# Expert weights in 2 MB transfers and paired slots, in a two-layer trunk kernel on one core

## The reference

```python
def reference(x, ...):
    for l in range(DEPTH):                      # DEPTH = 2
        h = rmsnorm(x, mix_norm_g[l])
        z = h @ w_in[l]                         # 1024 x 8192
        q, k, v, ch, cb, cc, ga, gc = jnp.split(z, offs, axis=-1)
        ...
        a = diff_attention(q, k, v, bias_dist, lam, lam_init, subln_g[l])
        c = short_gated_conv(ch, cb, cc, conv_w[l])
        merged = sigmoid(ga) * (a @ w_o_attn[l]) + sigmoid(gc) * (c @ w_o_conv[l])
        x = x + merged @ w_o[l]
        h = rmsnorm(x, ffn_norm_g[l])
        if l % 2 == 0:
            f = swiglu(h, dense_w_gate_up[0], dense_w_down[0])     # FF_DENSE = 2816
        else:
            logits = h @ router_w[0]
            top_v, top_i = lax.top_k(logits, 2)
            gates = jax.nn.softmax(top_v, axis=-1)
            for e in range(8):                                     # FF_EXPERT = 3584
                f = f + cw[:, e:e + 1] * swiglu(h, w_gu[e], w_down[e])
        x = x + f
    return rmsnorm(x, final_norm_g)
```

## Time and profile before

| What | Value |
|---|---|
| median of three runs | 1671.43 us |
| the profiled execution, its own time | 1670.79 us |
| its span in the profile | 1669.0 us |
| busy: PE, DVE, ACT | 98%, 79%, 66% |
| bytes moved, mean rate | 488.74 MB, 293 GB/s |
| start of the experts' first matmul, end of their last | 761.91, about 1653.5 us |
| TensorE's granted clock | full nearly throughout |

### The profile page before, as it was taken

One profiled execution on the slowest core, in us unless ns is written; L12 is line 12 of the kernel. 1 busy time (PEld: TensorE's weight loads), 2 busy tenths in 40 slices (PEclk: granted clock), 3 DMA queues, 4 the chain that ended last, 5 costly groups with the idle time before them and its releaser, 6 DMA issues.

```text
span 1669.0 us, 23179 instructions
## 1 busy us (share of the span) xinstructions
PE 1639.0 (98%) x8338; PEld 1373.9 (82%) x8338; DVE 1319.3 (79%) x1133; ACT 1102.0 (66%) x1076; POOL 225.6 (14%) x398
## 2 busy tenths in 40 slices
PE   9999999999999999999999999999999999999996
PEld 7988888888889888888888788887888887888875
DVE  6567656545465677468999999889999899998997
ACT  5355744444444557447768887778887688877885
POOL 0034440000000344407920000000000000000000
PEclk9999999999999999999999999999999999999998
DMA  8654544555545444536998999989999899999894
GB/s 339 264 177 152 187 179 164 202 184 193 179 173 177 169 159 171 188 147 254 412 379 348 417 421 401 409 334 397 421 398 418 348 374 419 419 399 379 341 422 199
DMA packets 71792, 488.74 MB, mean 293 GB/s; under 512 B 8651, under 2 KB 11932, under 8 KB 13212
## 3 DMA queue, kind: packets, MB, share of 16 engines
q1 hardware_dynamic: 69052, 483.89, 74.3%
q10 hardware_dynamic: 2656, 3.70, 0.7%
HBM read 484.94 MB, written 2.62 MB: 292 GB/s over the span
## 4 chain that ended last, share of the span: by engine, by line
PE 82%; DVE 9%; DMA 4%; issue 3%; ACT 1%; DVEq 0%; SPq 0%; ACTq 0%
PE bank L418 20%; PE bank L420 20%; PE bank L419 20%; DMA w_raw<-expert_slabs 3%; PE bank L1941 3%; PE bank L1942 3%; DVE w_lo L414 3%; PE bank L1722 3%; PE bank L1724 3%; PE bank L1725 3%; DVE e_v L411 2%; DVE e_uy L414 2%; PE bank L1920 2%; PE bank L1958 1%; DVE e_bias L414 1%
## 5 line engine op out<-in xcount | busy, mean ns | idle before, releaser
L414 DVE TENSOR_TENSOR w_lo<-w_raw,w_hi 128x2048 fp32r<-128x2048 f32 x288 | 654.5, 2292 | 210.2 <-ACT w_hi L405 209.8
L405 ACT ACTIVATE w_hi<-w_raw 128x2048 fp32r<-128x2048 f32 x288 | 551.2, 1918 | 389.3 <-PE bank L420 280.5
L418 PE MATMUL bank<-w_hi,hT 128*128 128x512 f32 x720 | 285.2, 396 | 1.9 <-DVE w_lo L1167 1.9
L420 PE MATMUL bank<-w_hi,hT 128*128 128x512 f32 x720 | 281.3, 391 | 0.0
L419 PE MATMUL bank<-w_lo,hT 128*128 128x512 f32 x720 | 280.8, 390 | 0.0
L418 PEld LDWEIGHTS bank<-w_hi,hT 128*128 128x128 f32 x720 | 135.5, 188 | 28.6 <-issue 2.1
L420 PEld LDWEIGHTS bank<-w_hi,hT 128*128 128x128 f32 x720 | 135.4, 188 | 28.7
L419 PEld LDWEIGHTS bank<-w_lo,hT 128*128 128x128 f32 x720 | 135.7, 188 | 26.8
L414 DVE TENSOR_TENSOR e_uy<-w_raw,e_k 128x2048 fp32r<-128x2048 f32 x56 | 128.2, 2288 | 16.7 <-ACT e_k L405 16.6
L411 DVE TENSOR_TENSOR e_v<-w_raw,hT 128x2048 fp32r<-128x2048 f32 x55 | 125.8, 2288 | 10.8 <-ACT hT L402 10.7
L405 ACT ACTIVATE e_k<-w_raw 128x2048 fp32r<-128x2048 f32 x56 | 107.5, 1920 | 34.3 <-PE bank L420 22.3
(11 more groups left out here) (355 smaller groups left out, 3125.9 us busy)
## 6 DMA issues: line engine op xcount, KB each, us to landing
w_raw<-expert_slabs SPq DMA_DIRECT2D x334, 1024.0 KB, 7.4
w_raw<-mix_slabs SPq DMA_DIRECT2D x88, 1024.0 KB, 4.8
w_raw<-dense_slabs SPq DMA_DIRECT2D x33, 1024.0 KB, 4.8
bias_lines<-bias ACTq DMA_DIRECT2D x1, 1536.0 KB, 7.5
X<-in_x SPq DMA_DIRECT2D x2, 512.0 KB, 5.8
bias<-bias_lines SPq DMA_DIRECT2D x1, 1024.0 KB, 6.8
yT<-in_ffn_norm_g ACTq DMA_DIRECT2D x2, 512.0 KB, 5.0
v_buf<-expert_slabs SPq DMA_DIRECT2D x1, 1024.0 KB, 4.7
```

What stands on the lines that cost most here:

```text
L405: act.activation(hi_slot(n), raw_of(n, early), ACT.Copy).then_inc(hi_ready, 1)
L414: eng.tensor_tensor(lo_slot(n), raw_of(n, early), hi_slot(n), ALU.subtract).then_inc(lo_ready, 1)
L418: pe.matmul(dst, hi, whi, start=first, stop=False, skip_group_check=True)
L420: return pe.matmul(dst, lo, whi, start=False, stop=last, skip_group_check=True)
```

## The change

Only the experts' stream changes its form; the mixers and the dense mixer still load halves. In the experts SP loads two halves with one transfer of 2 MB (`load_pair`) into two neighbouring slots of the same ring of six. ACT still makes the high parts half by half, but both wait for the one semaphore of the pair. DVE makes the low parts of both halves with one operation on 4096 floats a partition (`split_lo_pair`), which raises `lo_ready` by two. The slots of high and low parts become three pairs. `raw_slot` starts the experts' ring at slot 2. The loads into spare tiles in the opening are gone; the first pair is split in the mixer's last halves, the second behind the first gather. Beside this: the last dense step turns its last activations earlier and puts them in other tiles, `norm(2)` changes the order of two DVE operations, `rsqrt_of` loses one operation, and the end of the program works by halves of the columns, with the first rows scaled and sent by ACT.

```diff
-        w_hi = sb("w_hi", [P, SPLIT, HALF], F32R)
-        w_lo = sb("w_lo", [P, SPLIT, HALF], F32R)
+        w_split = sb("w_split", [P, 2 * SPLIT, HALF], F32R)
+        w_hi, w_lo = w_split[:, 0:SPLIT, :], w_split[:, SPLIT:2 * SPLIT, :]
...
+        moe_hi = (e_qv, w_split[:, 0:2, :], w_split[:, 2:4, :])
+        moe_lo = (e_bias, e_ku, w_split[:, 4:6, :])
...
+        def raw_slot(n):
+            return (n - MOE0 + 2) % RAW if n >= MOE0 else n % RAW
...
+        def load_pair(sp, n, src, cyc, opening=False):
+            at = raw_slot(n)
+            if opening and n < MOE0 + RAW:
+                sp.wait_ge(lo_ready, max(h for h in range(MOE0) if h % RAW in (at, at + 1)) + 1)
+            else:
+                sp.wait_ge(lo_ready, n - RAW + 2 + RAW * cyc)
+            sp.dma_start(w_raw[:, at:at + 2, :], src).then_inc(landed[at], 16)
...
         def split_hi(act, n, cyc=0):
+            slot, loads = raw_slot(n), n // RAW + 1
+            if n >= MOE0:
+                slot -= slot % 2
+                loads = loads_ahead(slot) + (n - MOE0) // RAW + 1
+            act.wait_ge(landed[slot], 16 * loads + 16 * cyc)
+            hi_slot_free(act, n, cyc)
+            act.activation(hi_slot(n), raw_of(n), ACT.Copy).then_inc(hi_ready, 1)
...
+        def split_lo_pair(eng, d, cyc=0):
+            def flat(pair):
+                return pair.rearrange("p h c -> p (h c)")
+
+            eng.wait_ge(hi_ready, MOE0 + 2 * d + 2 + RAW * cyc)
+            at = raw_slot(MOE0 + 2 * d)
+            eng.tensor_tensor(flat(moe_lo[d % SPLIT][:, :, :]), flat(w_raw[:, at:at + 2, :]),
+                              flat(moe_hi[d % SPLIT][:, :, :]), ALU.subtract).then_inc(lo_ready, 2)
...
@@ stream_expert, on SP
-                    load_half(sp, MOE0 + 3, gate_up(3, 0), CYCLES * b)
-                    for i in range(4):
-                        load_half(sp, MOE0 + 4 + i, gate_up(i, 1), CYCLES * b)
-                    with sp.Fori(2, MSTEPS) as m:
-                        load_step(m, CYCLES * b + m - 2)
+                for k in range(4):
+                    load_pair(sp, MOE0 + 2 * k, pair_of(e, 6 * (k // 2) + 2 * (k % 2)), CYCLES * b, opening)
+                with sp.Fori(2, MSTEPS) as m:
                     for i in range(2):
+                        load_pair(sp, MOE0 + 8 + 2 * i, pair_of(e, 6 * m + 2 * i), CYCLES * b + m - 2)
+                    load_pair(sp, MOE0 + 12, pair_of(e, 6 * (m - 2) + 4), CYCLES * b + m - 2)
...
@@ norm(q), on DVE
-                norm_lo(q, 0, 1)
+                if q != 2:
+                    norm_lo(q, 0, 1)
                 for hf in range(2):
                     add_sums(q, 1, hf)
                     raw_rows(q, 1, hf)
+                    if q == 2 and hf == 0:
+                        norm_lo(q, 0, 1)
...
@@ narrow_block, on DVE
-                    lo(c, 3, 4)
+                    lo(c, 1)
                     take_y(b)
-                    lo(c, 5, 6, 7, 8, 9)
+                    lo(c, 2, 3, 4)
                     fold_prod(b, i2, 0)
                     for i in range(3):
                         add_scattered(b, i)
                     fold_lo(b, 0, 0)
-                    lo(c, 10)
+                    lo(c, 5)
                     add_scattered(b, 3)
...
@@ the end, on ACT and DVE
-            for t in range(TT):
-                act.wait_ge(x_add, 4 * blocks + 2 * (t + 1))
-                act.activation(part[:, :], X[:, t, :], ACT.Square, accum_out=ssq[:, t:t + 1]).then_inc(ss_ready, 1)
+            for hf in range(2):
+                for t in range(TT):
+                    act.wait_ge(x_add, 4 * blocks + 2 * hf + t + 1)
+                    act.activation(part[:, 0:CHUNK], X[:, t, CHUNK * hf:CHUNK * (hf + 1)], ACT.Square,
+                                   accum_out=half_ss[:, hf, t:t + 1]).then_inc(ss_ready, 1)
...
+            act.activation(hrow[:, 0, :], hrow[:, 0, :], ACT.Copy, scale=rs[:, 0:1]).then_inc(out_scaled, 1)
+            act.dma_start(out[0, 0:P, :], hrow[:, 0, :]).then_inc(out_sent, 16)
...
+            dve.tensor_tensor(hrow[:, 0, :], X[:, 0, :], last_gain[:, :], ALU.mult).then_inc(gain_done, 1)
+            chain(dve.tensor_tensor(ssq[:, :], half_ss[:, 0, :], half_ss[:, 1, :], ALU.add))
             rsqrt_of(ssq[:, :], 1.0 / D)
+            dve.scalar_tensor_tensor(out=hrow[:, 1, :], in0=X[:, 1, :], scalar=rs[:, 1:2], in1=last_gain[:, :],
+                                     op0=ALU.mult, op1=ALU.mult).then_inc(hrow_ready, 1)
@@ the end of the dense mixer, on TensorE
-                down(n0 + DENSE_HALVES - 1, 0, FSTEPS - 1, closing=True)
+                down(n0 + 7, it, FSTEPS - 2, turned=FSTEPS - 1)
+                down_tile(n, FSTEPS - 1, 0, last_hi, last_lo).then_inc(sum_ps, 1)
+                down_tile(n, FSTEPS - 1, 1, last_hi, last_lo, closing=True).then_inc(half_used, 1)
```

More of the change, by code:

```diff
@@ L363, in one, with raw_of, loads_ahead @@
+        def raw_slot(n):
+            return (n - MOE0 + 2) % RAW if n >= MOE0 else n % RAW
+        def raw_of(n):
+            return w_raw[:, raw_slot(n), :]
+        def loads_ahead(slot):
+            return len(range(slot, MOE0, RAW))
         def one(slabs, at):
             return slabs[bass.ds(at, 1), :, :].rearrange("o p c -> (o p) c")
-        def load_half(sp, n, src, cyc=0, slot_free=False):
-            if n >= RAW and not slot_free:
-                sp.wait_ge(lo_ready, n - RAW + 1 + RAW * cyc)
-            sp.dma_start(w_raw[:, n % RAW, :], src).then_inc(landed[n % RAW], 16)
@@ L371, in load_early, with load_half, load_half_in @@
[L371 to L379 removed]
+        def load_half(sp, n, src):
+            if n >= RAW:
+                sp.wait_ge(lo_ready, n - RAW + 1)
+            sp.dma_start(raw_of(n), src).then_inc(landed[raw_slot(n)], 16)
+        def load_half_in(sp, n, src, cyc):
+            sp.wait_ge(lo_ready, n - RAW + 1 + RAW * cyc)
+            sp.dma_start(raw_of(n), src).then_inc(landed[raw_slot(n)], 16)
@@ L775, in mixer @@
                         split_hi(act, n0 + s + 2)
+                    if s == MIX_HALVES - 2 and layer == 1:
+                        split_hi(act, MOE0 + 1)
                     if s == 38 and layer == 1:
@@ L876, in silu, with turn_hi @@
                                        scale=rs[:, t:t + 1]).then_inc(d_silu, 1)
-                def turn_hi(m):
+                def turn_hi(m, last=False):
                     act.wait_ge(d_turn, m + 1)
-                    act.activation(ffT_hi, bank[2][:, :], ACT.Copy).then_inc(d_hi, 1)
+                    act.activation(ffT_hi if not last else last_hi, bank[2][:, :], ACT.Copy).then_inc(d_hi, 1)
                 n0 = DENSE0
@@ L1608, in experts @@
                 for i in range(4):
-                    add_scattered(blocks, i)
+                    t, hf = i % 2, i // 2
+                    cols = slice(CHUNK * hf, CHUNK * (hf + 1))
+                    dve.wait_ge(scatter_ps, 4 * blocks + i + 1)
+                    dve.tensor_tensor(X[:, t, cols], X[:, t, cols], bank[i][:, :], ALU.add).then_inc(x_add, 1)
+                dve.wait_ge(x_add, 4 * blocks + 4)
             def constants():
@@ L2061, in experts @@
                 blocks = last + 1
-                pe.wait_ge(y_lo_ready, 2 * blocks)
                 pe.wait_ge(spread_ready, 2 * blocks)
                 pe.wait_ge(x_add, 4 * blocks)
-                for i in range(4):
-                    scatter(blocks, i)
+                for hf in range(2):
+                    pe.wait_ge(y_lo_ready, 2 * blocks + hf - 1)
+                    for t in range(TT):
+                        cols = slice(CHUNK * hf, CHUNK * (hf + 1))
+                        pe.matmul(bank[2 * hf + t][:, :], spread_r[:, t, :], y_hi[:, cols], start=True, stop=False)
+                        pe.matmul(bank[2 * hf + t][:, :], spread_r[:, t, :], y_lo[:, cols], start=False,
+                                  stop=True).then_inc(scatter_ps, 1)
             pe.wait_ge(zero_ready, 1)
```

324 lines of the change are left out of this document (139 added, 185 removed).

## The result

The changed kernel takes 1840.47 us (median of 4 runs, 1832.72 to 1843.53) against 1671.7 us for the kernel before: a ratio of 1.1008, 95% interval 1.0982 to 1.1034. It is 169 us slower. The forecast was 1701 us, with a range to 1725. The direction was right; the loss is five and a half times the 31 us that were forecast.

What follows compares the result with a forecast made beforehand. TensorE bounds wide blocks; transfers and DVE nearly tie in narrow ones. Paired ring +34.6, opening +0.5, dense end -1.5, norm(2) -0.6, Newton -0.4, end -1.8: +30.8 on 1670.8, rounded to 1701 us; range 1663 to 1725.

Steps and rivals of the forecast that it cites:

- What bounds the kernel before: Experts: TensorE bounds wide blocks; in narrow ones DVE and transfers nearly tie, with 20 us above TensorE's need in all four.
- The spare 5.6 us of a turn: Ring of six halves before: 14.9 us between loads of a slot, 9.3 needed, so 5.6 spare.
- the turn of the paired ring: Experts' three 2 MB slots: landing 7.3, high parts 3.75, low part, hand-overs and small operations; 16.1 us, bounds 14.9 to 18.8.
- The narrow blocks: Experts' four narrow blocks: each 6.7 us longer than 99.9, together 26.8 us.
- Late starts: Wide blocks after narrow ones start 2.6 us late, three times, 7.8 us, otherwise hiding the ring's 5.37 us a pair.
- rival C: Experts: turn 18.0 us or more, 6.0 a pair, all 168 pairs pay: +116, 1785 us; 0.12 together with pairs wanted early.
- D: Wide blocks stall for a pair's second half, +12 us on the forecast; 0.12 together with the ring slower than wide blocks hide.
- The order of the low parts: Narrow block's opening: half 4 waits for half 5, halves 8 and 9 come 2.0 us later.
- The merged VectorE operation: Experts' low parts: merging two saves at most 0.08 x 168 = 13 us of DVE time; 0.4 us a narrow block, already counted.
- The small edits: Outside the experts' steady stream: opening +0.5, dense end -1.5, norm(2) -0.6, Newton chain -0.4, program's end -1.8 us.
- Size of the transfers: Experts' loads: the skill favours larger transfers, but 1 MB pieces already move 421 GB/s, the fixed part hidden by queueing.
- The test I wrote down: Profile after: narrow blocks 105 to 108 us, loads 5.3 us apart; wide-block TensorE waiting for low parts throughout means the slowest ring.

Runs made afterwards that it cites:

- the control: The kernel before without the third matmul of each product in the experts' wide blocks: 1636.01 us, ratio 0.9806.
- the ring alone: Separate kernel with only loads, high and low parts, no TensorE: three 2 MB slots take 6.08 us a pair with paired low parts, 5.33 with single ones.
- the fastest kernel: The changed kernel with 1 MB loads, low parts of one half each and the old order of low parts: 1665.47 us, 0.9973 to the kernel before.
- the unpaced rings: Separate kernels without TensorE: three 2 MB slots, high parts and paired low parts, no timing operation behind each low part: 5.8 to 6.1 us a pair.
- the third ring above: Separate kernel without TensorE: three 2 MB slots, first starts spaced 5.6 us, no timing operation behind the low parts: 5.99 us a pair.
- the clocked pattern: Separate kernel, 2 MB loads started by a clock at 4.1, 6.1, 8.1 us: those 8.1 behind their forerunner took 7.5 to 7.8 us.

## Why the prediction was wrong, step by step

**What bounds the kernel before: right, but its margin was not.** Wide blocks are TensorE's own and transfers and VectorE are near ties in the narrow ones; the control shows it, since wide blocks fall when TensorE has less to do. The spare 5.6 us of a turn (14.9 less 9.3) were wrong: a ring with one slot less loses 31 us at once. The 9.3 counts no wait of a slot for its place in the order on ScalarE and VectorE. The earlier trace rows had a sign of it: a landing of 8.2 us instead of 4.8 shows only 3.4 of the 5.6 as queueing, and 2.2 had gone elsewhere.

**The step that failed** is the turn of the paired ring, as the prediction put it: "I take 16.1 because the nearest row is the lone load: with a turn longer than the supply needs, little queues." The terms themselves were right: lone landing 7.3 (measured 7.3 to 7.7), two high parts 3.75 (3.71 to 3.72), low part 4.35 (4.43). "Little queues" was not: the landing in the ring was the term that failed. In the ring alone the loads land in 10.1 us, and the turn is 17.5 to 18.2; in the kernel it is 18.7 in the slot shown, 6.2 us a pair. Three loads that each hold the engines 5.6 need 16.8 us, more than my 16.1; what I took for room wasn't there. That is only part of the 10.1: what delays one load in three beyond it stays open (see the last section). The 18.8 that I had as the upper bound, from the 7.5 of the earlier trace rows, middle, was the nearer row: it is of loads in a ring, and the lone load isn't.

**The narrow blocks** got 25 to 32 us longer, not 6.7: 111 in the four instead of 26.8. **Late starts** of wide blocks (7.8) became 57 us of wide blocks longer throughout: at 6.2 a pair the ring is slower than the 5.86 that a wide block needs. This is rival C, whose condition I put as a turn of 18.0 or more and priced at 116 us for 6.0 a pair. The blocks took 1063 us for 168 pairs, 6.33 each, and lost 168. Together with D it had 0.12 of the chance, beyond 1722.

**The order of the low parts** was in the count as half 4's and halves 8 and 9's delay, 2.0 us at a narrow block's start, taken to be eaten up later by the ring. With single halves, where the ring has its room, the same order costs 7 us a narrow block and 2 a wide one, 33 in all.

**The merged VectorE operation** was priced rightly: 4.43 us against 4.50 for two in the ring alone. The 0.07 a pair are nothing beside the time by which it delays the slot's next load: in the ring alone a pair takes 6.08 us with it and 5.33 without, 2.2 us a turn. The Trainium skill, page "VectorE: DVE Perf Modes", section on the TRN2 errata, gives 4096 + 151 cycles, at its clock an estimate of 4.42 us: the duration agrees, but of the saving of 0.16 a pair that it implies only 0.07 is there, since two low parts in a row start 2.21 us apart and not 2.29.

**The small edits**, in the fastest kernel. Dense end and norm(2), -2.1 predicted: the Newton chain there starts at 477.64 instead of 479.48, -1.8 (476.52 in the changed kernel, -3.0). The opening, +0.5: block 0 is 0.7 shorter. The program's end, -1.8: from ScalarE's first result to the end of the span 14.4 us instead of 15.2, -0.8. The last scaling is 1.2 shorter (1.28 instead of 2.48), as counted, but from its end the two outputs, started together, need 4.3 us to the end of the span where the last one needed 3.2; I had 0.3 for that. A gain of some 2.5 us ahead of the first gather was not in my sum at all (below).

**Size of the transfers.** The Trainium skill, page "DMA: Bandwidth & Descriptors", section "Bandwidth", asks for at least 1 MB and shows larger ones faster; its table is for loads issued by GpSimd, and here SP issues them. For one transfer at a time the runs agree (221 GB/s for 1 MB, 287 for 2 MB). For a ring in the same memory they say the reverse: with single low parts 422 in six slots of 1 MB and 387 in three of 2 MB, and 345 in those with paired low parts.

**The test I wrote down** points to C: TensorE waits for low parts in the wide blocks too, idle for 9 us of block 4.

## What to carry to other kernels

A buffer ring is priced by its turn under load: landing measured in the ring, plus every operation that holds the slot, divided by the number of slots. Making pieces twice as big in the same memory halves the slots and lengthens each term at once, and a transfer that is large and alone was slower per byte (287 GB/s) than small ones that queue (422). Before trusting slack in a ring, take one slot away: here that one run (+31 us) would have shown that the counted slack was not there.

## What was not expected of the hardware

- A 2 MB load on idle engines holds them 5.6 us (busy share 0.62 at 231 GB/s), behind another 5.0 (422 GB/s). With even starts no wait shows at 5.6 us apart, at 5.1 the landing grows from 7.5 to 9.6.
- In the unpaced rings the landings of two loads in each bunch of three follow from that by arithmetic (landing of the forerunner plus 5.0 to 5.6). The first of a bunch often lands 1 to 3 us later still. In the third ring above, the load started at 746.50 lands in 10.1 us, 8.4 behind its forerunner; in the clocked pattern such a load took 7.5 to 7.8. From 745.5 to 748.0 the DMA share is only 0.59, while the forerunner lands at 748.76, so it is not that all engines were taken. Why stays open, and with it, by this arithmetic, the larger part of the miss in the landing time.
- TensorE's clock fell behind some of its stalls. In the kernel before the granted clock was 1.00 all through the experts; in the one after, behind an idle time of 4.3 us, eight matmuls started 0.43 us apart, the lower of its two levels (granted clock 0.52 from 797.2 to 800.7), before the spacing of 0.23 came back:

```profile
792.59 0.39 PE L423 MATMUL bank<-w_split,hT 128*128 128x512 f32 x1
797.26 0.72 PE L421 MATMUL bank<-e_qv,cT_hi 128*128 128x512 f32 x1 [4.29 <-DVE e_bias L416]
797.78 0.63 PE L422 MATMUL bank<-e_bias,cT_hi 128*128 128x512 f32 x1
798.20 0.63 PE L423 MATMUL bank<-e_qv,cT_lo 128*128 128x512 f32 x1
```

  The same 8338 instructions were busy 1690.9 us instead of 1639.0. Since the kernel with fewer matmuls gained next to nothing, those 52 us are most likely beside what bounds, not on it.
- Around the router the granted clock was at its lower level for longer in the kernel before (0.50 from 747 to 755) than in the one after (0.50 from 743 to 745, then 1.00 from 747 on) and in the fastest kernel (0.50 from 749 to 751). The twelve zero matmuls there took 5.23 us and now 2.98 (4.54 in the fastest kernel). From the router's first matmul to the first gather it is 16.2 us before, 13.7 after and 13.5 in the fastest kernel, about half of the gain of 5.2 ahead of the first gather. What made the clock come back sooner was not tried.

```profile
751.09 5.23 PE L1882 MATMUL bank<-zero_r 128*128 128x512 f32 x12
```

```profile
747.46 2.98 PE L1890 MATMUL bank<-zero_r 128*128 128x512 f32 x12
```
